# Fused transformer blocks, one core: the modulation rows are loaded into the weight ring instead of a buffer of their own

## The chip, the cores and the metric

The kernel is one program on one core of a Trainium2 chip. The metric is the device time of one execution in microseconds (us). The engines are named as in the profile: PE (TensorE, matmul), PEld (its weight load), DVE (VectorE), ACT (ScalarE), POOL (GpSimd), SP (SyncE, which here issues DMAs only). A wait on a semaphore holds everything that is queued behind it on its engine.

## The reference

Two blocks in a row in float32, on 512 tokens x and 256 context tokens with 1024 channels. The first has two layers: gated linear attention with differential attention, then a state-space mixer, each with a SwiGLU network and layer norms. The second has a SwiGLU network, a mixer of window attention and a gated scan (HGRN), and another SwiGLU network. Each layer's inputs are shifted, scaled and gated by "modulation" vectors, products of two conditioning vectors with a wide matrix:

```python
mod_x = jax.nn.silu(c) @ mod_w[layer] + mod_b[layer]          # 1024 -> 6144, two layers
mod_c = jax.nn.silu(c_ctx) @ mod_w[layer] + mod_b[layer]
hx = x * (1.0 + scm_x) + shm_x
mix_c, mix_x = even_mixer(hc, hx, ...) or odd_mixer(...)
x = layer_norm(ALPHA * x + gm_x * mix_x, ln_g[layer, 0], ln_b[layer, 0])
x = layer_norm(ALPHA * x + gf_x * swiglu(x * (1.0 + scf_x) + shf_x, ...), ln_g[layer, 1], ln_b[layer, 1])
...
mod = (jax.nn.silu(c) @ w_ada[l] + b_ada[l]).reshape(B, N_MOD, 1, D)   # 1024 -> 9216
```

## The kernel before, in words

Everything is written by hand. `plan` makes one list of 2756 steps; each engine walks the whole list and emits its share of every step, so the list fixes each engine's order. Waits are on semaphores.

**Weights.** A weight matrix is used in *panels* of at most 128 x 1024 float32 (512 KB), 475 of them. A panel is loaded into one of the four slots of the ring `RW` (panel n into slot n mod 4). For float32 accuracy from fp32r matmuls it is split: ACT copies it, rounded, to `RWH` ("hi", line 121), then DVE or POOL subtracts to get the rest, `RWr` ("lo", line 124). DVE does the panels with n mod 3 = 0, POOL the others. PE waits for the lo part before the first matmul of a panel. SP issues the load of panel n when PE has done with panel n-4, strictly in the order of n. `upto` says how far the splits and loads may run ahead at a step: at most 4 panels ahead for SP and 2 (`AHEAD`) for the splits, and only once panel n-4 is left behind in the list. Inside four latency-critical stretches ("calm") splits are held back further. A split stands in the order of ACT, DVE and POOL like any other instruction, and waits there.

**Modulation rows.** The 21 blocks of 1024 modulation values take 8 *rows* each, 168 in all (96 of `mod_w`, 72 of `w_ada`). A row is a 128 x 1024 piece of the matrix, 512 KB, used as it is, unsplit, by four matmuls with two output rows (`Mod.tensor`). PE does a row in about 0.6 us; the records show eight matmuls for it. After 8 rows ACT copies the sums out (`rowb`), PE turns them and DVE adds the bias ("turn"). Rows have a ring of their own, `MW`, three deep (class `Rows`): row n is issued by SP once row n-3 is used.

Where the rows stand in the list: 16 at the very start, before anything can be modulated; 8 in each of the two recurrent parts of the linear attention ("gla"); 16 in the differential attention; 14 around the layer norm before the first network, 42 between the panels of that network, 8 around the norm before the state-space mixer, 8 around the next norm, 8 in the second network, 8 around each of the two norms before and after the third network, 16 in the scan, 8 around the last norm. Around a norm, half the tokens' last products ("tail") alternate with the norm of the other half and with single rows (`ln_then_head`, `post_then_head`, line 3374 on); what is left of the rows stands in one run just before the *head*: the first two or three panels of the next stage, opened together. The head therefore begins when all of its panels are split.

Of the kernel before, what the change touches and what calls it, by code (L numbers as in the profile page):

```python
# [32 lines left out]
class Book:  # L33
# [3 lines left out]
    def __init__(self, make):  # L37
        self.make, self.sems, self.values, self.now, self.owner = make, {}, {}, {}, {}
# [34 lines left out]
class Eng:  # L73
# [2 lines left out]

    def __init__(self, who, real, k):
        self.who, self.real, self.k, self.book, self.seen, self.event = who, real, k, k.book, {}, None
        self.done_hi = self.done_lo = self.done_in = self.done_row = 0

    def wait_ge(self, name, *key):
        if self.real is None:
# [130 lines left out]
class Weights:  # L213
# [1 line left out]


    def __init__(self, k):
        self.k, self.specs, self.asked, self.used, self.through = k, [], 0, {}, []
        self.counting, self.left, self.calm = False, {}, {}

    def panel(self, p, nk, *cuts):

        n = self.asked
        self.asked += 1
        width = sum(w_ for _, w_ in cuts)
        assert nk * width <= 1024
        if self.counting:
            self.specs.append((nk, width, cuts))
        p.wait_ge(self.lo_name(n), n)
        fl = slice(0, nk * width)  # L230
        i = n % 4
        return n, *(x[:, i, fl].rearrange("p (k n) -> p k n", k=nk) for x in (self.k.RWH, self.k.RWL))

    def upto(self, i, ahead):


        n = self.through[i]
        while n < len(self.specs) and n < self.through[i] + 4 and ahead and self.left.get(n - 4, -1) < i - (
                self.calm.get(i, 0) if ahead < 4 else 0):
            ahead -= 1  # L240
            n += 1
        return n

# [3 lines left out]
    def fetch(self, y, upto):  # L247
        while y.done_in < min(upto, len(self.specs)):
            n = y.done_in
            y.done_in += 1  # L250
            nk, width, cuts = self.specs[n]
            if n >= 4:
                y.wait_ge(*self.used[n - 4])
            raw = self.k.RWF[:, n % 4, 0:nk * width].rearrange("p (k n) -> p k n", k=nk)
            at = 0
            for src, w_ in cuts:
                y.dma(raw[:, :, at:at + w_], src).then_inc(f"w.in{n % 4}", n, by=16)
                at += w_

    def split_hi(self, s, upto):  # L260
        while s.done_hi < min(upto, len(self.specs)):
            n = s.done_hi
            s.done_hi += 1
            nk, width, _ = self.specs[n]
            i, fl = n % 4, slice(0, nk * width)
            if n >= 4:
                s.wait_ge(*self.used[n - 4])
            s.wait_ge(f"w.in{i}", n)
            s.copy(self.k.RWH[:, i, fl], self.k.RWF[:, i, fl]).then_inc("w.hi", n)

    def split_lo(self, e, upto):
        while e.done_lo < min(upto, len(self.specs)):
            n = e.done_lo
            e.done_lo += 1
            if self.lo_name(n) != f"w.lo_{e.who}":
                continue
            nk, width, _ = self.specs[n]
            i, fl = n % 4, slice(0, nk * width)
            e.wait_ge("w.hi", n)
            e.tt(self.k.RWL[:, i, fl], self.k.RWF[:, i, fl], self.k.RWH[:, i, fl].bitcast(F),  # L280
                 ALU.subtract).then_inc(self.lo_name(n), n)


class Rows:

    DEEP = 3

    def __init__(self, k):  # L290
        self.k, self.src, self.step = k, [], {}

    def fetch(self, y, at):
        while y.done_row < len(self.src):
            n = y.done_row
            if n >= self.DEEP:
                if self.step[n - self.DEEP] >= at:
                    return
                y.wait_ge("pe.row", n - self.DEEP)
            y.done_row += 1  # L300
            y.dma(self.k.MW[:, n % self.DEEP, :], self.src[n]).then_inc(f"mw.in{n % self.DEEP}", n, by=16)


def wp(w, c0, n, r0=0, nk=8):
# [3 lines left out]
class Stage:  # L308


    def tensor(self, p, step, *a):
        pass
# [184 lines left out]
class Mod(Stage):  # L497
# [4 lines left out]
    def __init__(self, k):  # L502
        self.k = k
        a = k.a
        self.todo = [(a["mod_w"][0], k.M0, c, 0, "mod_b", 0) for c in range(6)]
        self.todo += [(a["mod_w"][1], k.M1, c, 0, "mod_b", 48) for c in range(6)]
        self.todo += [(a["w_ada_2"][0], k.M2, c, 1, "b_ada", 0) for c in range(9)]
        self.at, self.turned = 0, 0
        k.rows.src = [w[128 * kk:128 * kk + 128, 1024 * c:1024 * c + 1024] for w, _, c, _, _, _ in self.todo for kk in range(8)]

    def some(self, n, upto=168):

# [14 lines left out]
    def tensor(self, p, step, i):  # L527
        k = self.k
        if step == "row":
            b, kk = divmod(i, 8)  # L530
            w, _, c, x, _, _ = self.todo[b]
            if kk == 0:
                k.banks.take(p, 1, "mod", b)
            raw = k.MW[:, i % k.rows.DEEP, :]
            p.wait_ge(f"mw.in{i % k.rows.DEEP}", i)
            p.wait_ge("s.cs", x)
            for j in range(4):
                last = p.mm(k.banks.of("mod", b)[32 * j:32 * j + 2, 0:256], k.CS[:, x, kk, :],
                            raw[:, 256 * j:256 * j + 256], kk == 0, kk == 7)
            last.then_inc("pe.row", i)  # L540
        else:
            pt = k.banks.take(p, 1, "mod_t", i)
            p.wait_ge("s.row", i)
            for q in range(2):
                last = p.tr(pt[:, 128 * q:128 * q + 128], k.rowb[:, q * 128:(q + 1) * 128])
            last.then_inc("pe.row_t", i)
# [2781 lines left out]
def among(steps, extra, first=0, last=None):  # L3328

    last = len(steps) if last is None else last  # L3330
    out, at = [], 0
    for i, step in enumerate(steps):
        out.append(step)
        while first <= i < last and at < len(extra) * (i - first + 1) // (last - first):
            out.append(extra[at])
            at += 1
    return out
# [11 lines left out]
def run(stage, step, part, *tiles):  # L3349
    return [(stage, step, part, kk) for kk in tiles]  # L3350
# [95 lines left out]
def plan(k, out):  # L3446

    a, PX = k.a, (X, C)
    pro, mod, scale = Prologue(k), Mod(k), ModScale(k)
# [38 lines left out]
    steps = among(ffn.steps(), [("mod", 104)] * 42)  # L3488
# [13 lines left out]
    steps = among(ffn.steps(), [("mod", 128)] * 8)  # L3502
    steps = among(steps, run(ln, "late", H0, *range(8)) + run(ln, "late", H1, *range(8)), 2, 18)
# [51 lines left out]
    steps = []  # L3555
    for entry in order:
        steps += {"mod": lambda: mod.some(1, entry[1]), "mod_end": lambda: mod.until(entry[1])}.get(
            entry[0] if isinstance(entry[0], str) else "", lambda: [entry])()
    k.rows.step = {step[2]: i for i, step in enumerate(steps) if step[0] is mod and step[1] == "row"}
    for stage, names, n in ((diff, ("score",), 10), (ssd, ("cin", "yd"), 0), (hgrn, ("l2", "l3"), 24), (window, ("score",), 0)):  # L3560
        at = [i for i, step in enumerate(steps) if step[0] is stage and step[1] in names]
        k.w.calm.update((i, n) for i in range(at[0], at[-1]))
# [53 lines left out]
def sync_program(y, k, order, only=None):  # L3616
    for i in only or range(len(order)):
        stage, *step = order[i]
        if stage != "mark":
            stage.sync(y, *step)  # L3620
            k.rows.fetch(y, i)
            k.w.fetch(y, k.w.upto(i, 4))


# [18 lines left out]
def program(nc, a, con, out):  # L3643
    with ExitStack() as held:
        def sb(name, shape, dt=F):
            return held.enter_context(nc.sbuf_tensor(name, shape, dt))

        def sb2(name, shape):
            with nc.sbuf_tensor(name, shape, F) as f:
                pass  # L3650
            return f, sb(name + "r", shape, FR)
        k = Kernel()
# [4 lines left out]
        k.RWF, k.RWL = sb2("RW", [128, 4, 1024])  # L3657
        k.RWH = sb("RWH", [128, 4, 1024], FR)
        k.A, k.AR = sb2("A", [128, 18432])
        k.MW = sb("MW", [128, Rows.DEEP, 1024])  # L3660
        k.TM = sb("TM", [128, 4896])
        k.VEC = sb("VEC", [128, 5, 128])
        k.CS = sb("CS", [128, 2, 8, 2])
# [10 lines left out]
        PS = held.enter_context(nc.psum_tensor("PS", [128, 4096], F))  # L3674
        k.epsc, k.onec = k.cols[:, 0:1], k.cols[:, 1:2]
        k.ident, k.triF, k.triB, k.perm = (k.CC[:, i, :] for i in range(4))
        at = [0]
# [14 lines left out]
        k.acc = ([k.TM[:, 3072 + 512 * i:3584 + 512 * i] for i in range(2)], [k.TM[:, 4096:4352]])  # L3692
        k.sq_g = SqSet([k.TM[:, 4608:4864]], col(16))
        k.book = Book(lambda name: held.enter_context(nc.semaphore(name)))
        k.banks, k.w, k.rows, k.marks = Banks(PS), Weights(k), Rows(k), {}
        order = plan(k, out)

        count(k, order)
        block = held.enter_context(nc.Block())

        @block.sync
        def _(eng):
            sync_program(Eng("y", eng, k), k, order)
# [68 lines left out]
```

## Time and profile before

| | us |
|---|---|
| median of 3 runs | 4278.09 (4273.23 to 4280.25) |
| profiled execution | 4278.09 |
| its span | 4276.3 |
| PE busy in the span | 3870.9 (91%) |
| DVE, ACT, POOL busy | 1634.0, 1419.5, 1146.7 |
| mean granted clock of TensorE | 0.937 |

PE is busy for most of the span and carries most of the chain of waits; a change matters where PE waits. The DMA engines move 79 GB/s in the mean, in bursts around the norms.

### The profile page before, as it was taken

The page shows a single profiled execution, that of the slowest core. Times are in us where ns is not written, and L with a number is a line of the kernel's source. Part 1 is how long each engine was busy: PE and PEld are TensorE (multiplying, and loading weights), DVE is VectorE, ACT ScalarE, POOL GpSimd, SP SyncE. Part 2 cuts the span into 40 slices and gives each one's busy share as a digit, 9 for nine tenths or more (in the row PEclk, how much of TensorE's full clock was granted, in tenths as well). Part 3 has the DMA queues.
Part 4 walks back from the last instruction along what each step waited for, and adds up shares of the span by engine and source line. Part 5 has one row for each costly group of instructions (what it writes and reads, how often), then busy time and mean ns, then how long its engine had stood idle before and what let it go on. Part 6 is the DMA issues. An engine that isn't in the chain of part 4 may idle for free.

```text
span 4276.3 us, 52557 instructions
## 1 busy us (share of the span) xinstructions
PE 3870.9 (91%) x22131; PEld 3232.9 (76%) x22131; DVE 1634.0 (38%) x2831; ACT 1419.5 (33%) x2221; POOL 1146.7 (27%) x713
## 2 busy tenths in 40 slices
PE   5989878999998888888899989999978889898999
PEld 3767756888887677777778878888867676587888
DVE  2344454111135655646621241011247745332113
ACT  3222444212125223232432352221245535443223
POOL 1100003111123224231522341211333423243323
PEclk8989989999998898989899989999979989899999
DMA  4221124333332010111243332222232211143333
GB/s 160 69 76 40 40 79 128 99 104 99 104 113 75 25 50 30 50 36 45 79 123 108 100 114 68 65 65 65 74 108 60 60 46 38 33 123 99 95 98 109
DMA packets 471926, 336.69 MB, mean 79 GB/s; under 512 B 17530, under 2 KB 445580, under 8 KB 471692
## 3 DMA queue, kind: packets, MB, share of 16 engines
q1 hardware_dynamic: 471691, 333.34, 25.7%
q8 instruction: 175, 2.87, 0.3%
q14 instruction: 60, 0.48, 0.0%
HBM read 331.20 MB, written 2.10 MB: 78 GB/s over the span
## 4 chain that ended last, share of the span: by engine, by line
PE 76%; DVE 10%; ACT 4%; POOL 3%; DMA 3%; issue 3%; SPq 0%; POOLq 0%; DVEq 0%; ACTq 0%
PE PS L107 75%; DVE A L132 2%; PE PS L115 2%; DVE A L124 2%; DMA MW<-in_mod_w 1%; POOL RWr L124 1%; POOL TM L124 1%; ACT RWH L121 1%; DVE TM L132 1%; ACT A L118 1%; POOL A L124 1%; DVE TM L124 1%; ACT L118 1%; DVE RWr L124 1%; DVE XT L124 0%
## 5 line engine op out<-in xcount | busy, mean ns | idle before, releaser
L124 POOL TENSOR_TENSOR RWr<-RW,RWH 128x1024 fp32r<-128x1024 f32 (+2 forms) x316 | 725.3, 2297 | 2342.6 <-ACT RWH L121 2342.1
L107 PE MATMUL PS<-HTH,RWH 128*128 128x512 f32 (+3 forms) x3376 | 1222.0, 362 | 38.9 <-DVE HTr L124 14.1
L107 PE MATMUL PS<-HTr,RWH 128*128 128x512 f32 (+3 forms) x3376 | 1194.6, 354 | 0.0
L107 PE MATMUL PS<-HTH,RWr 128*128 128x512 f32 (+3 forms) x3376 | 1192.7, 353 | 0.0
L107 PE MATMUL PS<-Ar,RWH 128*128 128x512 f32 (+1 forms) x3264 | 828.1, 345 | 18.7 <-POOL Ar L124 8.7
L107 PEld LDWEIGHTS PS<-HTH,RWH 128*128 128x128 f32 (+2 forms) x3376 | 652.0, 193 | 164.5 <-issue 54.6
L107 PEld LDWEIGHTS PS<-HTH,RWr 128*128 128x128 f32 (+2 forms) x3376 | 650.6, 193 | 88.1 <-issue 1.3
L107 PEld LDWEIGHTS PS<-HTr,RWH 128*128 128x128 f32 (+2 forms) x3376 | 652.8, 193 | 82.3 <-issue 1.7
L107 PEld LDWEIGHTS PS<-Ar,RWH 128*128 128x128 f32 x3264 | 569.6, 193 | 111.2 <-issue 30.3
L121 ACT ACTIVATE RWH<-RW 128x1024 fp32r<-128x1024 f32 (+3 forms) x475 | 475.6, 1005 | 407.8 <-DMA RW<-in_ffn_w_out 180.2
L107 PE MATMUL PS<-Ar,RWr 128*128 128x512 f32 (+1 forms) x1632 | 556.5, 341 | 0.0
L124 DVE TENSOR_TENSOR A<-A,PS 128x512 f32<-128x512 f32 (+2 forms) x192 | 139.0, 724 | 820.4 <-PE PS L107 786.6
L124 DVE TENSOR_TENSOR RWr<-RW,RWH 128x1024 fp32r<-128x1024 f32 (+3 forms) x159 | 203.5, 1280 | 634.6 <-ACT RWH L121 634.5
L107 PE MATMUL PS<-A 128*128 128x128 f32 (+5 forms) x1692 | 326.5, 358 | 70.8 <-DVE A L124 32.5
L107 PEld LDWEIGHTS PS<-Ar,RWr 128*128 128x128 f32 x1632 | 315.0, 193 | 34.3
L107 PEld LDWEIGHTS PS<-A 128*128 128x128 f32 (+1 forms) x1692 | 233.3, 211 | 133.7 <-issue 68.5
L118 ACT ACTIVATE A<-PS 128x768 f32<-128x768 f32 (+2 forms) x148 | 93.0, 631 | 559.1 <-PE PS L107 549.7
L121 ACT ACTIVATE Ar<-A 128x512 fp32r<-128x512 f32 (+2 forms) x132 | 90.9, 689 | 546.6 <-DVE A L124 527.8
L132 DVE SCALAR_TENSOR_TENSOR XT<-PS,M,XT 128x512 f32<-128x512 f32 (+1 forms) x200 | 118.9, 619 | 337.1 <-PE PS L107 337.1
L118 ACT ACTIVATE A<-A 128x512 f32<-128x512 f32 (+4 forms) x144 | 103.1, 729 | 321.6 <-DVE A L132 146.8
L121 ACT ACTIVATE A<-PS 128x256 f32<-128x256 f32 (+5 forms) x200 | 104.0, 545 | 298.8 <-PE PS L107 217.8
L118 ACT ACT_TABLE_LOAD x137 | 175.8, 1283 | 34.0 <-PE PS L107 31.0
(181 smaller groups left out, 3783.2 us busy)
## 6 DMA issues: line engine op xcount, KB each, us to landing
RW<-in_ffn_w_in SPq DMA_DIRECT2D x176, 512.0 KB, 3.8
MW<-in_mod_w SPq DMA_DIRECT2D x96, 512.0 KB, 4.7
MW<-in_w_ada SPq DMA_DIRECT2D x72, 512.0 KB, 4.4
RW<-in_ffn_w_out SPq DMA_DIRECT2D x64, 512.0 KB, 3.7
RW<-in_ffn_w_out SPq DMA_DIRECT2D x64, 384.0 KB, 3.2
RW<-in_mix_w_in SPq DMA_DIRECT2D x41, 512.0 KB, 3.8
RW<-in_ssd_w_in SPq DMA_DIRECT2D x40, 512.0 KB, 4.0
RW<-in_ev_w_in SPq DMA_DIRECT2D x24, 512.0 KB, 3.9
```

What stands on the lines that cost most here:

```text
L107: return self._ins(self.real and self.real.matmul(o, l, r, start=start, stop=stop, skip_group_check=True))
L115: return self._ins(self.real and self.real.transpose(o, i, self.k.ident[0:n, 0:n]))
L118: return self._ins(self.real and self.real.activation(o, i, f, **kw))
L121: return self._ins(self.real and self.real.activation(o, i, ACT.Copy))
L124: return self._ins(self.real and self.real.tensor_tensor(out=o, in0=i0, in1=i1, op=op))
L132: return self._ins(self.real and self.real.scalar_tensor_tensor(out=o, in0=i0, scalar=sc, in1=i1, op0=op0, op1=op1))
```

## The change

The ring `MW` and the class `Rows` go. A row is now a "plain" panel of the ring `RW`: it takes the next number, its slot, its place in SP's order, and is not split. Panels and rows together are 643 entries. A plain entry doesn't count against the two or four entries that a split or load may run ahead, but it holds its slot. Which engine makes the lo part still goes by n mod 3, with the new numbers: 155 panels on DVE instead of 159, 320 on POOL instead of 316. The last edit drops an argument that sets the size of a DMA scratch area.

```diff
+    def whole(self, p, src, width):
+        n = self.asked
+        self.asked += 1
+        if self.counting:
+            self.specs.append((1, width, ((src, width),)))
+            self.plain.add(n)
+        p.wait_ge(f"w.in{n % 4}", n)
+        return n, self.k.RWF[:, n % 4, 0:width]
...
         n = self.through[i]
         while n < len(self.specs) and n < self.through[i] + 4 and ahead and self.left.get(n - 4, -1) < i - (
                 self.calm.get(i, 0) if ahead < 4 else 0):
-            ahead -= 1
+            ahead -= n not in self.plain
             n += 1
...
+            if n in self.plain:
+                continue
...
-            if self.lo_name(n) != f"w.lo_{e.who}":
+            if n in self.plain or self.lo_name(n) != f"w.lo_{e.who}":
                 continue
...
-class Rows:
...
-    DEEP = 3
...
-    def fetch(self, y, at):
-        while y.done_row < len(self.src):
...
-            raw = k.MW[:, i % k.rows.DEEP, :]
-            p.wait_ge(f"mw.in{i % k.rows.DEEP}", i)
+            num, raw = k.w.whole(p, w[kk * 128:kk * 128 + 128, c * 1024:c * 1024 + 1024].rearrange(
+                "(k p) n -> p k n", k=1), 1024)
             p.wait_ge("s.cs", x)
...
             last.then_inc("pe.row", i)
+            k.w.used[num] = ("pe.row", i)
...
-            k.rows.fetch(y, i)
             k.w.fetch(y, k.w.upto(i, 4))
...
-        k.MW = sb("MW", [128, Rows.DEEP, 1024])
...
-    nc = _bacc.Bacc("TRN2", target_bir_lowering=False, num_devices=1, dynamic_dma_scratch_size=1024)
+    nc = _bacc.Bacc("TRN2", target_bir_lowering=False, num_devices=1)
```

PE's order is the same but for the buffer's name. ACT's order at the start of the program, before (-) and now (+): `XT` are the tokens, `RWH` the hi part of a panel, `rowb` the sums of eight rows.

```order
-L121 ACTIVATE RWH<-RW 128x256
-L121 ACTIVATE RWH<-RW 128x1024
 L118 ACTIVATE XT<-PS 128x512 x8
 L118 ACTIVATE XT<-PS 128x256 x8
-L121 ACTIVATE rowb<-PS 2x256 x8
+L121 ACTIVATE rowb<-PS 2x256 x4
+L121 ACTIVATE RWH<-RW 128x256
+L121 ACTIVATE RWH<-RW 128x1024
+L121 ACTIVATE rowb<-PS 2x256 x4
```

The first two splits stood ahead of the tokens' copies; they now stand between the two blocks' sums.

SP's order before the first network (norm "f0"), before the change: `in_ev_w_out` is the tail, `in_ffn_w_in` the head and the network, `in_mod_w` the rows.

```order
L104 DMA RW<-in_ev_w_out 128x2x512 x2
L104 DMA MW<-in_mod_w 128x1024
L104 DMA RW<-in_ev_w_out 128x2x512
L104 DMA MW<-in_mod_w 128x1024 x5
L104 DMA RW<-in_ev_w_out 128x2x512
L104 DMA MW<-in_mod_w 128x1024 x5
L104 DMA RW<-in_ffn_w_in 128x8x128 x2
L104 DMA MW<-in_mod_w 128x1024 x3
L104 DMA RW<-in_ffn_w_in 128x8x128
```

The same place now:

```order
L104 DMA RW<-in_mod_w 128x1024 x10
L104 DMA RW<-in_ev_w_out 128x2x512 x3
L104 DMA RW<-in_mod_w 128x1024 x4
L104 DMA RW<-in_ev_w_out 128x2x512
L104 DMA RW<-in_mod_w 128x1024 x10
L104 DMA RW<-in_ffn_w_in 128x8x128 x2
L104 DMA RW<-in_mod_w 128x1024
```

The head's two panels were issued with ten or more rows still to come; they are now issued after the last of them.

SP's order before the second network (norm "f1"), before the change: `in_ssd_w_out` is the tail, `in_w_ada` the rows.

```order
L104 DMA RW<-in_ssd_w_out 128x4x256 x8
L104 DMA MW<-in_w_ada 128x1024
L104 DMA RW<-in_ffn_w_in 128x8x128
L104 DMA MW<-in_w_ada 128x1024 x2
L104 DMA RW<-in_ffn_w_in 128x8x128
L104 DMA MW<-in_w_ada 128x1024 x2
```

And now:

```order
L104 DMA RW<-in_ssd_w_out 128x4x256 x5
L104 DMA RW<-in_w_ada 128x1024 x2
L104 DMA RW<-in_ssd_w_out 128x4x256
L104 DMA RW<-in_w_ada 128x1024 x2
L104 DMA RW<-in_ssd_w_out 128x4x256
L104 DMA RW<-in_w_ada 128x1024 x2
L104 DMA RW<-in_ssd_w_out 128x4x256
L104 DMA RW<-in_w_ada 128x1024 x2
L104 DMA RW<-in_ffn_w_in 128x8x128 x8
```

The tail's panels were all issued ahead of the rows; now two rows stand before each of the last three, and all rows before the head.

## Rows read from the trace of the kernel before

**Rows 1.** The page's chain that ended last, share of the span by engine

```profile
PE 76%; DVE 10%; ACT 4%; POOL 3%; DMA 3%; issue 3%; SPq 0%; POOLq 0%; DVEq 0%; ACTq 0%
```

**Rows 2.** Instructions that use MW, whole span: who waited (us, times), and the landings

```profile
  PEld PS L107: 60.1, 28
  PE PS L107: 41.5, 27
...
DMA to landing us min/median/max: 3.4/4.5/12.1
```

**Rows 3.** Timeline, 9 to 64 us: start, length, engine, operation, count [idle before <-releaser]

```profile
25.08 1.06 ACT L121 ACTIVATE RWH<-RW 128x1024 fp32r<-128x1024 f32 x1 [1.37 <-DMA RW<-in_ev_w_in]
...
26.68 3.86 PE L115 MATMUL PS<-CC,A 128*128 128x128 f32 x16 [5.03 <-ACT XT L118]
...
30.46 1.48 PE L107 MATMUL PS<-MW,CS 128*2 128x256 f32 x24
31.14 28.33 SPq L104 DMA_DIRECT2D MW<-in_mod_w  x16
35.05 0.61 PE L107 MATMUL PS<-MW,CS 128*2 128x256 f32 x8 [3.11 <-DMA MW<-in_mod_w]
36.30 0.61 PE L107 MATMUL PS<-MW,CS 128*2 128x256 f32 x8 [0.64 <-DMA MW<-in_mod_w]
...
59.14 1.53 ACT L121 ACTIVATE rowb<-PS 2x256 f32<-2x256 f32 x4 [14.15 <-PE PS L107]
```

**Rows 4.** Timeline of PE, linear attention's recurrence, first block and second

```profile
148.19 1.03 PE L107 MATMUL PS<-MW,CS 128*2 128x256 f32 x8 [4.15 <-DMA MW<-in_mod_w]
...
149.16 2.08 PE L107 MATMUL PS<-A 64*128 64x256 f32 x8
...
152.98 1.13 PE L107 MATMUL PS<-A 64*128 64x256 f32 x8
...
156.52 0.61 PE L107 MATMUL PS<-MW,CS 128*2 128x256 f32 x8 [1.86 <-DMA MW<-in_mod_w]
...
280.35 1.03 PE L107 MATMUL PS<-MW,CS 128*2 128x256 f32 x8 [3.36 <-DMA MW<-in_mod_w]
```

**Rows 5.** First network, 700 to 1260 us: groups, then DMA issues to landing

```profile
L124 POOL TENSOR_TENSOR RWr<-RW,RWH 128x1024 fp32r<-128x1024 f32 x37 | 88.6, 2393 | 405.9 <-ACT RWH L121 405.9
...
L121 ACT ACTIVATE RWH<-RW 128x1024 fp32r<-128x1024 f32 x56 | 58.9, 1051 | 114.4 <-DMA RW<-in_ffn_w_out 64.3 <-DMA RW<-in_ffn_w_in 50.0
...
L124 DVE TENSOR_TENSOR RWr<-RW,RWH 128x1024 fp32r<-128x1024 f32 x19 | 23.2, 1222 | 92.9 <-ACT RWH L121 92.9
...
RW<-in_ffn_w_in SPq DMA_DIRECT2D x40, 512.0 KB, 3.9
```

**Rows 6.** Timeline of PE around the norm f0, 655 to 691 us

```profile
661.69 0.28 PE L107 MATMUL PS<-Ar,RWr 128*128 128x256 f32 x1
...
663.90 0.61 PE L107 MATMUL PS<-MW,CS 128*2 128x256 f32 x8
664.44 0.50 PE L107 MATMUL PS<-Ar,RWH 128*128 128x256 f32 x2
...
676.81 1.03 PE L107 MATMUL PS<-MW,CS 128*2 128x256 f32 x8
...
689.70 0.80 PE L107 MATMUL PS<-HTH,RWH 128*128 128x512 f32 x1
```

**Rows 7.** Timeline of PE: first matmuls of two of the state-space norm's tail panels

```profile
1273.14 0.50 PE L107 MATMUL PS<-Ar,RWH 128*128 128x256 f32 x2
...
1294.60 0.50 PE L107 MATMUL PS<-Ar,RWH 128*128 128x256 f32 x2
```

**Rows 8.** Timeline around the head after the norm f1, 2103 to 2114 us

```profile
2105.24 0.61 PE L107 MATMUL PS<-MW,CS 128*2 128x256 f32 x8
...
2105.92 1.53 ACT L121 ACTIVATE rowb<-PS 2x256 f32<-2x256 f32 x4 [2.42 <-PE PS L107]
...
2110.67 1.99 ACT L121 ACTIVATE RWH<-RW 128x1024 fp32r<-128x1024 f32 x2
...
2113.33 0.55 PE L107 MATMUL PS<-HTH,RWH 128*128 128x256 f32 x1 [6.84 <-DVE RWr L124]
```

**Rows 9.** Stretches: us, busy of the engines, granted clock of PE, DMA share, GB/s

```profile
690.00:1260.00 570.00, 564.30 (x3360) 475.92 (x3360) 109.26 (x152) 131.01 (x176) 108.69 (x53) 1.00 0.31 99
```

More of the change, by code:

```diff
@@ L78, in __init__ @@
         self.who, self.real, self.k, self.book, self.seen, self.event = who, real, k, k.book, {}, None
-        self.done_hi = self.done_lo = self.done_in = self.done_row = 0
+        self.done_hi = self.done_lo = self.done_in = 0
     def wait_ge(self, name, *key):
@@ L217, in __init__ @@
     def __init__(self, k):
-        self.k, self.specs, self.asked, self.used, self.through = k, [], 0, {}, []
+        self.k, self.specs, self.asked, self.used, self.through, self.plain = k, [], 0, {}, [], set()
         self.counting, self.left, self.calm = False, {}, {}
+    def whole(self, p, src, width):
[6 more added lines that the diff above has]
+        return n, self.k.RWF[:, n % 4, 0:width]
     def panel(self, p, nk, *cuts):
@@ L281, in split_lo @@
                  ALU.subtract).then_inc(self.lo_name(n), n)
-class Rows:
-    DEEP = 3
-    def __init__(self, k):
-        self.k, self.src, self.step = k, [], {}
-    def fetch(self, y, at):
-        while y.done_row < len(self.src):
[L295 to L301, printed above, removed]
 def wp(w, c0, n, r0=0, nk=8):
@@ L508, in __init__ @@
         self.at, self.turned = 0, 0
-        k.rows.src = [w[128 * kk:128 * kk + 128, 1024 * c:1024 * c + 1024] for w, _, c, _, _, _ in self.todo for kk in range(8)]
     def some(self, n, upto=168):
@@ L3558, in plan @@
             entry[0] if isinstance(entry[0], str) else "", lambda: [entry])()
-    k.rows.step = {step[2]: i for i, step in enumerate(steps) if step[0] is mod and step[1] == "row"}
     for stage, names, n in ((diff, ("score",), 10), (ssd, ("cin", "yd"), 0), (hgrn, ("l2", "l3"), 24), (window, ("score",), 0)):
@@ L3694, in program @@
         k.book = Book(lambda name: held.enter_context(nc.semaphore(name)))
-        k.banks, k.w, k.rows, k.marks = Banks(PS), Weights(k), Rows(k), {}
+        k.banks, k.w, k.marks = Banks(PS), Weights(k), {}
         order = plan(k, out)
```

## The prediction

> **What bounds the kernel now.** The page's chain first: three quarters of it are PE [rows 1]. So an edit counts where it makes PE wait or stops it waiting, and DMAs, splits and copies count only if PE stands for them. Next, who waits for the rows: PE 41.5 us in 27 waits, with landings of 3.4 to 12.1 us, median 4.5 [rows 2]. The weight loads' figure beside it is mostly the same idle time seen from PEld, and isn't added. In the timeline these waits lie where rows stand close together: 12.4 us in the first 16 rows, 10.9 us in the linear attention, and the rest in the runs of rows in front of heads. Last, the stretch table: in the first network PE is busy for 564.3 of 570 us at full granted clock [rows 9]; there is nothing to win there, only to lose. The profiled execution took 4278.09 us, 1.8 us more than its span, and is the median of the three runs, so changes are added to it directly.
>
> **The price of a slot.** Everything below uses one chain, from PE's last use of a slot to the first matmul of the panel that takes it: SP's issue 0.2 us (SP's row at 31.14 follows PE's first row, 30.46 plus 0.5, by that), landing 3.9, hi part 1.05, lo part 2.4 on POOL or 1.2 on DVE [rows 3, 5], and 0.3 for three semaphores, my estimate from the same rows. That is 7.85 us with POOL, 6.65 with DVE. A row needs 4.1. Loads issued together land 1.25 us apart (36.30 minus 35.05) [rows 3]. Before, four panels were in this chain beside three rows; now four entries of both kinds are.
>
> **The start: -10.** Before, ACT's first two splits stood ahead of the tokens' copies. ACT waited for their panels until 25.08, PE for ACT 5.03 us, so its last transposes ran from 26.68 and the first row at 30.46 [rows 3]. Now no split stands there. PE's 32 transposes of x ended at 26.68 - 5.03 = 21.65; eight steps for the context follow at 0.3 us each, so rows begin at about 24.1. That is 6.4 us sooner, and four rows are there instead of three. Row 4 is issued at 24.9, lands at 29, and rows 5 to 7 land 1.25 us apart, at 32.9. Then PE waits 2.3 us for the turn, as before. Rows 8 to 11 are there by then; rows 12 to 15 land from 41.0 to 44.8. The last sum is ready at 45.5 instead of 59.1: -13.6. But between the two `rowb` copies ACT now has two splits. The second's panel is issued once row 13 is used (42.9) and lands at about 47.9; with the copy that makes 49.0, so 3.5 us come back: -10. Bounds -14 (ACT isn't held up) and -5 (the panels land later than rows do; before, the second came only just ahead of 25.08).
>
> **Linear attention: -7.** The rows stand in pairs there. Before, the fourth row waits 4.15 us, as only three were loaded ahead, and after this wait the row takes 1.03 us and the next eight matmuls 2.08 instead of 1.13; the eighth waits 1.86. The second block repeats it (3.36 for the fourth row) [rows 4]. With four slots the fourth row is loaded when the last panel before it is done, at about 140.7, and comes 1.4 us late; the fifth and sixth are late by 1 us each. So 3.5 to 4 of each block's 5 to 6 us go. Bounds -11 (all waits go) and -3. The panel behind the last pair takes the slot of the fifth row; its 7.85 us end just when PE arrives.
>
> **The norm f0: +12.** Read [rows 6] by slots. Tail panel A, last used at 661.69 + 0.28 = 661.97, is followed by row r4 (663.90) in its slot: r4 lands at 661.97 + 4.1 = 666.1, late by 2.2. Panel B (wanted at 664.44) has the slot of an earlier row but stands behind r4 in SP's order: it lands at 667.3, and with hi and POOL is ready at 670.9, another 4.2 late. r8 (676.81) has B's slot; B ends at 676.9 + 6.4 = 683.3, so r8 comes at 687.4, 4.2 late. Six rows follow in one run; they waited 5.1 us before, and with r8's delay and four slots they still end near 695. The head's panels have the slots of the third- and second-last but one of them: the first is ready at 699.5, the second, on POOL too, at 702.0. PE began the head at 689.70: +12.3. Low bound +6: PE had small waits for the other half's norm in the head, and the norm's own chain may hide part. High bound +17: ACT stands behind B's split for 3 to 4 us with the first half's norm behind it.
>
> **State-space norm: +6.** Tail panels of 384 KB alternate with rows, seven first matmuls from 1273.14 to 1294.60, so one per 3.58 us [rows 7]. Now two panels and two rows fill the ring, so two panels take 2.4 us of matmuls and a chain of about 6.3 (0.2, 3.2, 0.8, 1.8 and 0.3, scaled by size from [rows 5]): 4.35 per panel. That is 0.8 x 6 = 4.6; the head's second panel adds 1 to 2. Bounds +3 and +9.
>
> **The norm f1: +9.** Two rows between the last tail panels: the panel wanted at about 2095.5 has the slot of the row that ends at 2090.9 and needs 7.85 us: 3 late; its neighbours about 1.5 and 0.7: +5. The head then hangs on ACT: last row 2105.24, `rowb` 2105.92, four norm copies, two splits 2110.67, DVE, head at 2113.33 [rows 8]. The first of these splits now stands ahead of `rowb` and its panel, in the slot of the last tail panel (2105.3), lands at 2109.4; `rowb` starts at 2110.5 instead of 2105.9. Hence +4 to +5. Bounds +3 and +13.
>
> **Norms b1, mix2, b2: +4, +4, +3.** Each has a run of five or six rows and then a head of two or three panels in these rows' slots. From the third-last row's end the second panel needs 7.85 us, in which the two remaining rows take 2.5: 5.3, less about 1 which the fourth slot saves in the run. b2's head already waited for a split of its third panel, so less. Bounds +1 and +7 each. **The scan:** 16 rows as singles; one panel's split is now placed one step ahead of its use, behind ACT's and DVE's backlog (+2, bounds 0 and +5), and the 2.5 us of waits for rows there shrink (-1). **Differential attention:** a stall of 3 us before a wait of equal length for ACT, 0 (bounds 0 and +4).
>
> **The first network: 0.** 42 rows between panels. With 56 wide splits in 560 us [rows 5] a panel lasts at most 10 us, by the stretch table some 8.5. At the 17 tightest places the slot's last use and the new panel's turn have one panel and two rows between them, 8.5 + 1.2 = 9.7 against 7.85. Slack 1.8 us, so nothing. DVE/POOL shares, four panels moved: 0. The scratch argument: it sets a reserve for another way of issuing than SP's, and all loads here are SP's: 0.
>
> **Sum.** -10 - 7 - 1 = -18; 12 + 6 + 9 + 4 + 4 + 3 + 2 = +40. 4278 - 18 + 40 = **4300 us**.
>
> **A rule of the skill on the chain.** The landing row says 3.9 us for 512 KB [rows 5]. The Trainium skill (DMA: Bandwidth & Descriptors, Anatomy of one DMA) gives, for loads issued by GpSimd, about 2.0 us fixed plus the bytes at 436 GB/s, an estimate of 3.2 us for this load. By it each of some twelve stalls would be 0.7 us shorter, and the sum about 4292; the trace has even its quickest row at 3.4, so I keep 3.9. The spacing of 1.25 us agrees with that bandwidth (1.2).
>
> **Rivals.** (1) *The stalls cost clock too.* After a wait of 4.15 us a row takes 1.03 us instead of 0.61 and eight matmuls 2.08 instead of 1.13, so some 1.4 us more per such wait [rows 4]. Six new waits of that size in the tails: +8, 4308. Against it: in the tails before, some matmuls already ran at the lower clock, and half my waits are shorter. The Trainium skill (TensorE: Matmul & The Clock Gate, Part 1: The HAM clock gate) has idle gaps drop the engine from 2.4 to 1.2 GHz; the trace's two durations agree. Chance 0.13. (2) *The ring is short in the first network as well*: ACT's or POOL's other work uses up the 1.8 us at the 17 places, 1 to 1.5 us each: +20, 4320. For it: ACT is now held for the landing there, with evictions behind it. Against: 114.4 us of ACT's idle time there was waiting for DMA anyway [rows 5]. Chance 0.10. (3) *Stalls hidden by the norms*: PE would have stood for the other half's norm anyway, as at the 6.84 us before f1's head [rows 8]. If half the +40 goes: 4280. Against: that wait's chain itself begins with the last row and its split. Chance 0.17. (4) *Faster.* The start and the linear attention give their bounds (-14, -11) and the stalls at the heads stay under +15, because the norms before the heads, not the ring, end last: 4278 - 25 + 15 = 4268. It decides at +16 of stalls (4269). Against it: f0 alone is 6 at its least. Chance 0.08. (5) That the change doesn't do what it says: SP's order shows that it does. The forecast keeps 0.52.
>
> **Range and chances.** A measurement of this kernel tells about 0.2% (8.6 us) from no change. 4300 with terms moving together spans 4286 to 4312; (1) and (2) reach beyond it above, (3) below. 4276 to 4318 leaves out half of (2), most of (4) and little else. Slower by over 0.2% (above 4286.6): 0.50 of the forecast, (1), (2) and a little of (3), 0.75. Faster by over 0.2% 0.08, within 0.17.
>
> **What would show it.** The first row of PE at about 24 us, the attention's first product some 10 us sooner; PE's waits before the fourth row in the linear attention down to 1 to 2 us. In the tails: PE's matmuls of panels with waits for POOL RWr or DVE RWr, ACT's RWH with waits for DMA RW of 2 to 5 us; each head's first matmul later against its last row than before. In 700 to 1260 us PE still over 98% busy. I am wrong if the heads' distances are unchanged (then 4 holds), or if PE waits for RWr all through the first network (2).

## The result, and the profile after

The kernel after takes 4319.56 us (median of 4 runs, 4318.03 to 4333.61), the kernel before 4275.66 in the same comparison. The ratio is 1.0116 with a 95% interval of 1.0085 to 1.0149: 36 to 64 us slower. The forecast was 4300. The ratio rests on three more executions of after besides these four; all seven lie between 4313.16 and 4345.09. The profiled execution of after is the slowest of the four (span 4331.1); a second trace of the same order of work, taken in experiment e13, has a span of 4319.8 and is read beside it.

The page's chain answers to [rows 1]; PE's share is one point lower, DVE's one higher:

```profile
PE 75%; DVE 11%; ACT 4%; DMA 3%; POOL 3%; issue 3%; SPq 0%; POOLq 0%; DVEq 0%; ACTq 0%
```

Who waits for `RW`, whole span (it holds the rows now, so this is not the same set as [rows 2]):

```profile
  PEld PS L107: 142.7, 62
  PE PS L107: 105.4, 48
...
DMA to landing us min/median/max: 2.7/3.8/12.9
```

The start, for [rows 3] (timeline: start, length, engine, operation, idle before and its releaser):

```profile
23.26 1.91 PE L107 MATMUL PS<-RW,CS 128*2 128x256 f32 x32
28.01 0.61 PE L107 MATMUL PS<-RW,CS 128*2 128x256 f32 x8 [2.85 <-DMA RW<-in_mod_w]
...
46.70 0.42 ACT L121 ACTIVATE RWH<-RW 128x256 fp32r<-128x256 f32 x1 [12.27 <-DMA RW<-in_ev_w_in]
48.41 1.06 ACT L121 ACTIVATE RWH<-RW 128x1024 fp32r<-128x1024 f32 x1 [1.29 <-DMA RW<-in_ev_w_in]
49.49 1.53 ACT L121 ACTIVATE rowb<-PS 2x256 f32<-2x256 f32 x4
```

The first row comes at 23.26 instead of 30.46, the second `rowb` at 49.49 instead of 59.14. The first network answers to [rows 9] and is unchanged:

```profile
702.00:1272.00 570.00, 564.42 (x3365) 476.19 (x3365) 109.72 (x153) 137.06 (x178) 111.99 (x54) 1.00 0.34 98
```

So the time is in the norms: f0, the state-space norm and f1, then b1 (before the third network), mix2 (before the last mixer) and b2 (before the last network). The stretch view over the six of them, cut at the same instructions in both kernels (from the first matmul of the tail's second half to the head's first or, for the state-space norm, last tile), shows it best. The columns that matter are the length, PE busy with its count, and the granted clock (third from the end). Before:

```profile
644.93:689.70 44.77, 36.74 (x252) 23.98 (x250) 27.58 (x42) 15.87 (x24) 22.71 (x18) 0.84 0.59 185
1268.64:1326.38 57.74, 49.02 (x330) 38.79 (x328) 30.16 (x48) 27.59 (x45) 29.91 (x24) 0.86 0.46 139
2056.63:2113.33 56.70, 44.85 (x328) 38.50 (x329) 29.91 (x60) 22.92 (x39) 33.86 (x28) 0.80 0.45 149
2490.74:2523.46 32.72, 23.01 (x184) 17.13 (x185) 8.42 (x20) 14.14 (x28) 15.42 (x15) 0.87 0.59 182
3100.99:3135.47 34.48, 28.98 (x204) 23.77 (x205) 14.03 (x20) 16.01 (x28) 17.92 (x12) 0.80 0.59 183
3848.08:3879.93 31.85, 22.75 (x201) 19.36 (x201) 10.85 (x20) 15.27 (x32) 16.29 (x13) 0.84 0.48 149
```

After:

```profile
635.82:701.69 65.87, 40.97 (x252) 27.98 (x250) 23.68 (x39) 15.09 (x23) 20.83 (x17) 0.68 0.44 144
1279.49:1342.79 63.30, 49.60 (x330) 38.66 (x328) 29.94 (x47) 28.51 (x46) 32.60 (x25) 0.87 0.43 125
2069.54:2144.11 74.57, 50.48 (x329) 42.94 (x329) 29.51 (x59) 22.85 (x40) 35.98 (x29) 0.73 0.37 113
2522.48:2565.70 43.22, 28.43 (x184) 22.17 (x185) 8.48 (x19) 17.34 (x34) 15.52 (x16) 0.65 0.55 161
3145.43:3192.10 46.67, 33.82 (x205) 27.84 (x205) 17.47 (x27) 17.66 (x29) 19.52 (x13) 0.67 0.46 125
3892.76:3934.55 41.79, 25.47 (x200) 21.59 (x200) 10.95 (x19) 17.19 (x36) 16.89 (x14) 0.76 0.53 151
```

The six last 258.3 us before and 335.4 after, 77.2 more. For the same matmuls PE is busy 205.4 us before and 228.8 after: 23.4 of the 77.2 is slower work, at a clock of 0.65 to 0.76 instead of 0.80 to 0.87 in five of six; 53.8 is waiting. In the second trace of this order the same sums are 322.9 and 221.3: 64.6 more, 16.0 of it slower work and 48.6 waiting. Outside the norms 21 to 22 us come back in both traces.

Where the same PE work starts in each trace, against before's trace, gives a ledger by part (us later; e14 and e15 have the rows of f0 or f1 alone in the ring, e5 and e1 are the kernel after with five and seven slots):

| part | forecast | after | e13 | e14 | e15 | e5 | e1 |
|---|---|---|---|---|---|---|---|
| up to f0's tail | -17 | -9.1 | -14.6 | +2.5 | -2.7 | -22.3 | -27.5 |
| f0 | +12 | +21.1 | +18.8 | +17.6 | -0.6 | +11.4 | +11.9 |
| first network | 0 | -1.1 | -1.2 | +0.4 | +0.2 | +0.5 | +1.4 |
| state-space norm | +6 | +5.5 | +5.9 | -1.1 | +0.1 | -1.3 | -3.2 |
| state-space stage | 0 | -3.5 | -3.5 | +0.1 | -0.8 | -19.6 | -17.3 |
| f1 | +9 | +17.9 | +16.5 | +0.1 | +15.1 | +17.4 | +7.8 |
| b1 | +4 | +10.5 | +6.4 | +1.1 | +4.9 | +3.2 | +0.2 |
| mix2 | +4 | +12.2 | +6.8 | -0.4 | -0.1 | +6.0 | +3.9 |
| scan, window | +1 | -11.9 | -6.3 | -0.1 | -3.1 | +2.6 | +1.4 |
| b2 | +3 | +9.9 | +10.2 | +0.4 | -0.1 | +3.2 | +6.9 |

The columns e14 and e15 also show how far a part without an edit moves from one execution to the next: mostly 1 us, up to 5. The second and third network (after +0.9 and +2.2) are left out. A norm's term can be cut once more, at the end of its last row. What is added behind it, up to the head's first matmul, is in after and e13 7.0 and 7.9 us at f0, 4.4 and 4.1 at f1, 8.3 and 6.6 at b1, 7.8 and 7.2 at mix2, 4.2 and 3.7 at b2; the rest of each term lies in the tail.

The chain through f0 says why its term grew (start, length, what; for [rows 6]):

```profile
659.25 2.35 POOL RWr L124
661.60 0.04 issue
661.65 15.70 PE PS L107 x80
677.34 0.02 issue
677.36 4.15 DMA RW<-in_mod_w
...
682.65 4.45 DMA RW<-in_mod_w
...
687.61 7.74 DMA RW<-in_ffn_w_in
...
695.71 1.06 ACT RWH L121
696.77 0.07 issue
696.84 4.65 POOL RWr L124 x2
```

The rows land after 4.15 and 4.45 us, as reckoned; the head's panel, issued behind rows, after 7.74 where 3.9 was reckoned. It is so at the head of b1 (DMA issues, 2545 to 2562 us: KB each, median us to landing), where the same form in the network has 3.9 [rows 5]:

```profile
RW<-in_ffn_w_in SPq DMA_DIRECT2D x4, 512.0 KB, 7.5
RW<-in_w_ada SPq DMA_DIRECT2D x3, 512.0 KB, 3.7
```

At f1, for [rows 8] (timeline):

```profile
2123.04 0.80 PE L107 MATMUL PS<-Ar,RWH 128*128 128x256 f32 x2 [4.35 <-POOL RWr L124]
...
2135.55 1.06 ACT L121 ACTIVATE RWH<-RW 128x1024 fp32r<-128x1024 f32 x1 [7.71 <-DMA RW<-in_ffn_w_in]
2136.51 1.51 ACT L121 ACTIVATE rowb<-PS 2x256 f32<-2x256 f32 x4
...
2144.11 0.55 PE L107 MATMUL PS<-HTH,RWH 128*128 128x256 f32 x1 [11.14 <-DVE RWr L124]
```

The split stands ahead of `rowb` and waits for its load, as foretold; from the last row (2131.22) to the head are 12.9 us instead of 8.1. The other 13 us of f1 are in its tail.

### The profile page after: what moved, and what is told of

Read it like the earlier page. It is cut to its first block, busy times and chain, and to the rows that moved or that the text cites. A ratio compares the mean times of both kernels' runs of the same rounds, so it can differ in the third digit from the quotient of the medians.

```text
span 4331.1 us, 52592 instructions
## 1 busy us (share of the span) xinstructions
PE 3884.8 (90%) x22131; PEld 3244.0 (75%) x22131; DVE 1647.4 (38%) x2827; ACT 1426.7 (33%) x2221; POOL 1156.3 (27%) x717
## 4 chain that ended last, share of the span: by engine, by line
PE 75%; DVE 11%; ACT 4%; DMA 3%; POOL 3%; issue 3%; SPq 0%; POOLq 0%; DVEq 0%; ACTq 0%
PE PS L107 73%; DVE A L124 3%; DVE A L132 2%; PE PS L115 2%; POOL RWr L124 1%; POOL TM L124 1%; DMA RW<-in_mod_w 1%; DMA RW<-in_ffn_w_in 1%; ACT RWH L121 1%; DVE TM L132 1%; POOL A L124 1%; DVE TM L124 1%; ACT A L118 1%; DVE RWr L124 1%; DVE SM L144 0%
## 5 line engine op out<-in xcount | busy, mean ns | idle before, releaser
L124 POOL TENSOR_TENSOR RWr<-RW,RWH 128x1024 fp32r<-128x1024 f32 (+3 forms) x320 | 733.0, 2293 | 2438.2 <-ACT RWH L121 2432.7
L107 PE MATMUL PS<-Ar,RWH 128*128 128x512 f32 (+1 forms) x3264 | 838.9, 348 | 35.8 <-POOL RWr L124 17.6
L107 PEld LDWEIGHTS PS<-Ar,RWH 128*128 128x128 f32 x3264 | 579.2, 196 | 131.9 <-issue 26.3
L124 DVE TENSOR_TENSOR RWr<-RW,RWH 128x1024 fp32r<-128x1024 f32 (+2 forms) x155 | 199.9, 1290 | 648.4 <-ACT RWH L121 648.2
L118 ACT ACT_TABLE_LOAD x137 | 175.8, 1283 | 36.3 <-PE PS L107 33.2
```

What stands on the lines that cost most here:

```text
L107: return self._ins(self.real and self.real.matmul(o, l, r, start=start, stop=stop, skip_group_check=True))
L118: return self._ins(self.real and self.real.activation(o, i, f, **kw))
L124: return self._ins(self.real and self.real.tensor_tensor(out=o, in0=i0, in1=i1, op=op))
```

## The experiments

The theories: **A**, rows hold slots that panels need. **B**, one queue in strict order costs, whatever the depth. **C**, the lo parts' new engines. **D**, ACT and POOL stand at splits with the norm's work behind them. **Q**, loads queue behind loads. Differences below are in us against the kernel before on the same chip, from the ratio, with its 95% interval.

**e1, seven slots.** The hi buffers stay four, taken in turn by panels alone, and the scratch argument is as before in e1 and e5 (e13 shows that it is worth nothing). Of the edit the lines that set the number are shown; the rest makes the slot `n % RING` (e5 has `RING = 5`).

```diff
+RING = 7
...
-        k.RWF, k.RWL = sb2("RW", [128, 4, 1024])
+        k.RWF, k.RWL = sb2("RW", [128, RING, 1024])
```

> The kernel after, with seven slots for the raw data of the shared ring (the memory that the row buffer had), and still four hi buffers, which the panels alone take in turn. One numbering and one order of loads stay. Theory A (too few slots: every row in a tail or a head's run takes a slot that a panel's load needed) expects that the loss of 44 us goes and the gain at the start and in the linear attention stays: 4258 to 4272, and the heads' first matmuls as far behind the last row as before. Theory B (one queue of loads in strict order of use is what costs, however many slots) expects 4300 or more. Theory C (which engine makes the lo part, since the numbers changed) expects 4305 to 4325.

Measured: 4260.12, **-10.7** (-15.4 to -6.4). With the memory of the row buffer put into the ring the loss in time is gone, though numbering and order are those of after. B and C fall as the main cause of it. But the loss in the norms is not gone, as the sums of the stretch view over the six of them show, first e5 (below), then e1:

```profile
sum 298.27, PE 209.94 PEld 165.81 DVE 119.77 ACT 117.25 POOL 135.77; mean PE 34.99 PEld 27.63 DVE 19.96 ACT 19.54 POOL 22.63
sum 285.77, PE 213.38 PEld 169.28 DVE 121.04 ACT 113.52 POOL 138.69; mean PE 35.56 PEld 28.21 DVE 20.17 ACT 18.92 POOL 23.11
```

Against 258.3 before, the norms are 27.5 us longer with seven slots and 40.0 with five, where four cost 65 to 77. The kernel is faster all the same because 27.5 us are won ahead of f0 and 17.3 in the state-space stage (ledger). The heads' first matmuls are again as far behind the last row as before at f1, mix2 and b2, as expected, but not at f0 (12.8 us more) and b1 (6.2 more). The chain of e1 into the head of f0:

```profile
653.41 9.14 DMA RW<-in_ffn_w_in
...
662.64 0.04 ACT RWH L122
...
663.60 0.81 ACT HTH L119
...
671.64 2.32 POOL RWr L125
```

The panel is issued early and lands late, behind other loads (Q), and the norm's copy `HTH` stands behind its split on ACT (D). More slots cure neither.

**e5, five slots.**

> The kernel after with five slots for the raw data instead of four (seven gave 4260). Theory A (a panel's load waits for a slot that a row holds): the tails, where panels and rows alternate one to one, need one slot more, and the heads' panels are issued one row sooner; well over half of the 60 us between four and seven slots come back: 4275 to 4290. If the loss were spread evenly over the three slots, 4300.

Measured: 4278.08, **+1.3** (-3.8 to 6.0). Against the runs' own comparisons the first slot more brings 42 to 48 us and the next two together 12 (by the bare times 42 and 18). A holds for the greater part: one slot more takes 25 to 37 us off the norms, most of it in the tails, and adds 8 to 13 to the lead ahead of f0. The 16 us more in the state-space stage have no experiment.

**e2, the lo part's engine by the count of panels.** The edit: `lo_name` counts panels without the rows.

> The kernel after, with the lo part's engine chosen by the count of panels alone, as before the change (159 on DVE, 316 on POOL, the same panels as before). Theory C (both panels of the first network's head fell to POOL, 4.6 us in a row instead of 2.4 beside 1.2): 3 to 8 us of the 44 come back, 4312 to 4317. Theory A: 4316 to 4322, the panels come late because of their slots and the engine of the lo part moves only some of the heads.

Measured: 4322.06, **+50.8** (41.9 to 59.4). C falls for the whole.

**e3, splits stand later.**

```diff
-            ahead -= n not in self.plain
+            ahead -= 1 if split else n not in self.plain
```

> The kernel after, with rows counted against the two entries that a split may stand ahead of its use: the splits of a head stand behind more of the rows and of the norm's own work in the order of ACT, POOL and DVE; loads are issued as in the kernel after. Theory D (ACT and POOL stand in front of a split whose load has just been issued, and the norm's squares and copies queue behind it: the half of the loss that the prediction did not have): 4295 to 4308. Theory A (the load itself is late): 4318 to 4330, since a split that stands later cannot be ready sooner.

Measured: 4315.14, **+45.3** (36.3 to 54.7), the loss of after within the interval. That speaks against D only where the edit moved a split, which is outside the norms and in the tails from the state-space norm on. Around f0 the order of ACT, DVE and POOL in the trace is that of after, and at f1, b1, mix2 and b2 two splits still stand ahead of `rowb`. ACT at the head of f1 in e3:

```profile
2131.48 1.06 ACT L121 ACTIVATE RWH<-RW 128x1024 fp32r<-128x1024 f32 x1 [6.62 <-DMA RW<-in_ffn_w_in]
2132.45 1.52 ACT L121 ACTIVATE rowb<-PS 2x256 f32<-2x256 f32 x4
```

So D was not tested at the heads, and there the traces show it at work: in after `rowb` begins 4.3 us behind the end of the last row at f1, 4.0 at mix2 and 4.3 at b2, each time held by a split that waits for its load; before it was 0.1. That is all that the heads of f1 and b2 lose and half of what mix2's loses.

**e4, e8, e10, the first rows alone.** Only rows below 32 or 16 go through `whole`, the others keep `MW`; in e10 the lo parts keep their engines of before too.

> The kernel before, with only rows 0 to 31 (start and linear attention) in the weight ring; all the others keep their own buffer of three. All theories: the gain of the first part alone. By the prediction 17 us (10 at the start, 7 in the linear attention), 4259; by the trace of the kernel after 10 to 11 us (the linear attention's gain was given back behind its second block), 4265. If the loss of 44 us sits in the tails and heads alone, this one is faster than before; if the shared ring costs in the linear attention too, 4266 to 4270.

> The kernel before, with only rows 0 to 15 (the start) in the weight ring (rows 0 to 31 gave 4258). The prediction has 10 us for the start and 7 for the linear attention; the traces have the start at 10 and next to nothing for the linear attention, where DVE's chain takes the place of the rows that are no longer waited for (PE waits 5 to 8 us for it in the second block). By the prediction 4263 to 4265; by the traces 4257 to 4260, the same as with rows 0 to 31.

> Rows 0 to 31 in the weight ring as in the run with 4258, with the lo part's engine chosen by the count of panels alone, so that every panel has the engine that it has in the kernel before. Theory S: 4256 to 4260 as with the shifted numbers. Theory N: 4264 to 4269, of which the start and the linear attention are all.

Measured: e4 4257.62, **-15.4** (-21.4 to -9.4); e8 4271.31, **-3.4** (-8.6 to 1.7); e10 4264.38, **-8.1** (-14.1 to -2.6). With every lo part on its engine of before, the start and the linear attention together are worth 8 (3 to 14), not 17. e4's other 7 are not clear of the noise; in its trace they lie in the state-space stage (-14.1 against e10's -1.9) and the scan, so they may belong to the shifted lo parts. e8 missed its expectation, and its gain is not clear of nothing. That not all of the linear attention's waits are won is seen in the chain of the kernel after through its second recurrence:

```profile
271.92 5.04 DMA RW<-in_ev_w_in
...
277.04 1.06 ACT RWH L121
278.10 0.02 issue
278.12 0.03 DVE RWr L124
...
280.21 0.34 DVE A L132
```

The panel behind the last pair of rows has a row's slot; DVE stands at its lo part until 278.12, with the recurrence's own steps queued behind it, and PE then waits 5.17 us for `A`. Before, it did not wait there. With seven slots (e1) the same wait is 7.69 us.

**e9, e12, the turn of DVE and POOL by itself.** `n % 3 == 1` or `== 2` in the kernel before.

> The kernel before, but DVE makes the lo part of the panels with n mod 3 = 1 instead of 0 (158 panels against 159); nothing else. Rows 0 to 31 in the ring gave 15 us, rows 0 to 15 gave 4, while in their traces both start equally early; what differs behind the linear attention is the numbers alone, shifted by 32 (so DVE has what was n mod 3 = 1) and by 16 (n mod 3 = 2). Theory N (the turn of DVE and POOL matters in the scans and the state-space stage, and the shifted numbers gave the rest): 4262 to 4268. Theory S (the turn is of no account, the linear attention is what made the 11 us): 4272 to 4280.

> The kernel before, but DVE makes the lo part of the panels with n mod 3 = 2 instead of 0; nothing else. It is the turn that panels behind the start have with rows 0 to 15 in the ring (4271). Theory N: this turn costs against that of before, 4279 to 4285, and explains why the start alone brought 4 and not 9 us. Theory S: 4272 to 4280.

Measured: e9 4272.46, **-4.7** (-9.0 to -0.4); e12 4276.66, **+0.9** (-4.7 to 6.0). Over the whole kernel the turn is worth little. In a part of it it can be worth more, as the next pair shows.

**e6, e14, f0's rows alone**, with shifted and with unshifted lo parts.

> The kernel before, with only rows 48 to 61 (the tail and head at the norm before the first network) in the weight ring. The trace of the kernel after has PE 21.6 us later over this stretch, where the prediction had 12. If the stretch by itself costs this, 4273 + 20 = 4293 (4288 to 4298); if half of it is only the start's gain given back (other engines were not earlier than before, so that PE waits for them again), 4273 + 12 = 4285.

> The kernel before with rows 48 to 61 in the weight ring, and every panel's lo part on its engine of before. If the term of f0 was right (12): 4288 (4284 to 4290). If it was mis-sized as the traces have it (17 to 21, since the head's panels land after 7.7 us): 4293 to 4297.

Measured: e6 4284.63, **+10.7** (6.8 to 14.5); e14 4299.23, **+22.7** (17.1 to 28.2). In the traces f0 itself costs nearly the same, 19.8 and 17.6 us. e6's trace gets 21 back in the state-space norm and stage, the third network and the scan, e14's nothing; 8 of the 21 is that e6's traced execution is its fastest (4276.43, median 4284.63). So e6's time, which seemed to confirm the term of 12, did so by other parts. The term is 17 to 21.

**e16, f0's rows with a quarter of the bytes** (the rest of each is left out).

```diff
+            if n in self.plain:
+                y.dma(raw[:, :, 0:256], cuts[0][0][:, :, 0:256]).then_inc(f"w.in{n % 4}", n, by=16)
+                continue
```

> As the run with rows 48 to 61 in the ring and the lo parts by the panel, but these 14 rows load only their first 256 of 1024 columns; the rest of each is left out. Theory Q (half of f0's cost is loads that stand in the queue behind other loads): 7 to 10 us less than with whole rows, 4284 to 4288. Theory A alone (slots held): 2 to 3 us less, from three rows that land 0.9 us sooner each.

Measured: 4289.06, **+15.0** (9.4 to 20.1), 7.7 less than e14; the f0 part itself is 12.5 instead of 17.6. The chains ahead of the head, e14 and then e16:

```profile
689.47 6.89 DMA RW<-in_mod_w
696.36 0.04 issue
696.41 0.66 PE PS L107 x8
697.06 0.02 issue
697.08 7.86 DMA RW<-in_ffn_w_in
```

```profile
683.24 2.12 DMA RW<-in_mod_w
...
691.86 6.10 DMA RW<-in_ffn_w_in
```

Rows land in 2.12 instead of 3.7 to 6.9, and the chain goes through the second head panel (6.10) instead of the first (7.86). Q holds for the rows' bytes: by the time in full, by the trace (5.1 us less at f0, where A alone had 2 to 3) in part. But the head's panels still land 6.6 us after issue in the median in both: they queue behind each other as well, which shorter rows don't change.

**e7, the same for all rows from 32 on.**

> The kernel after, but rows 32 to 167 load only their first 256 of 1024 columns (128 KB instead of 512), and PE multiplies these four times; the rest of each row is left out. The slots are held as before and the order is the same. Theory Q (in a run before a head the loads of rows and panels stand in one burst, so that the head's panels land after 7.4 us and not after the 3.9 of the network): the panels land sooner by the bytes of the two to three rows ahead of them, and the rows by their own 0.9 us each: 18 to 28 us of the 60 come back, 4292 to 4302. Theory A alone (slots, with landings of 3.9): only the rows' own landing gets shorter, some ten waits by 0.9: 4308 to 4313.

Measured: 4301.03, **+26.1** (20.5 to 31.6), so 18 to 24 less than after: Q's number. Here too the head's panels land after 5.6 to 6.0, not 3.9.

**e11, the runs ahead of four heads alone.**

> The kernel before, with only the rows that stand in one run ahead of the heads of f0, b1, mix2 and b2 in the weight ring (6, 6, 5 and 5 rows), and the lo parts on the engines of before. By the prediction the heads are 4 (b1), 4 (mix2), 3 (b2) and some 4 of f0's 12: 4275 + 15 = 4290. By the trace of the kernel after, whose head panels land 6.4 to 7.7 us after their issue instead of 3.9, each has 3 to 4 us more: 4275 + 28 = 4303 (4297 to 4308).

Measured: 4287.53, **+10.3** (5.6 to 15.0); in the trace f0 3.9, b1 2.7, mix2 6.4, b2 2.6, together 15.6. The number is the prediction's 15 and not my corrected 28, but it is so by two errors that cancel. From the last row to the head's first matmul PE loses 5.6, 6.1, 7.8 and 4.0 us, 23.5 together and nearly what the full change loses there (27.3 and 25.4 in its two traces), with first landings of 6.3 to 7.3 us in the chains; and the work up to the last row takes 7.9 us less than before in all (here the other rows still have their three slots, so there are more slots in all; that this is the reason is not tested). What the full change adds at these norms lies ahead of the last row, where single rows stand in the tails.

**e15, f1's rows alone.**

> The kernel before with rows 112 to 119 (the tail at f1) in the weight ring, lo parts on their engines of before. If the term of f1 was right (9): 4285. If it is as the trace of the kernel after has it (18): 4294. With the last tail panel's lo part on DVE, as here, and not on POOL as there, the trace with lo parts by the panel had 10: I take 4286.

Measured: 4291.05, **+19.7** (13.3 to 26.1), 15.1 in the part itself by the trace. Its chain has a tail panel that lands after 6.73 us behind the rows. The 4.9 us at b1, where nothing was edited, are slower work: PE is busy 29.8 us there instead of 23.0, at a clock of 0.62.

**e13, the scratch argument restored in the kernel after.**

> The kernel after with the argument for the DMA scratch area restored: this part alone is undone. All theories: no difference, 4320 (4314 to 4325), since every load is SP's. If the argument did cost something, 4310 or less. Its trace is a second one of the same order of work: f0 17 to 21 us, f1 10 to 18 by it, or the first trace misled.

Measured: 4319.32, **+43.2** (35.5 to 50.4), the time of after. This part of the change does nothing to the time.

**e17, e18, versions meant to be fast**: DVE's turn moved by one from row 48 on, with e10's and with e1's ring.

> Rows 0 to 31 in the weight ring, lo parts by the count of panels as in the run with 4264, but from row 48 on DVE has the panels with count mod 3 = 1. If the turn behind f0 is worth what the two pairs of runs show (7 and 14 us): 4250 to 4258. If it is not: 4262 to 4267. Faster than both kernels either way.

> Seven raw slots shared by rows and panels (4260), lo parts by the count of panels, from row 48 on with count mod 3 = 1 on DVE. If the turn is worth 7 to 14 us over that of before, and the turns of the run with seven slots were a mixture: 4250 to 4258; else 4260 to 4265.

Measured: e17 4257.91, **-21.8** (-28.3 to -15.8), faster than both kernels and the best against its own comparison, though its interval overlaps e4's; e18 4270.90, **-9.8** (-13.7 to -6.0), no better than e1. So the turn is no rule that carries over, and why it moves the state-space stage and the scan stays open.

## Why the prediction was wrong

The direction and the places were right, the size was half. By its steps:

- **Start, -10**: the trace has it (-9.7; `rowb` at 49.49 against about 49 foretold). In time the first 16 rows alone bring 3.4 (-8.6 to 1.7, e8) and the first 32 together 8.
- **Linear attention, -7**: failed. That the panel's 7.85 us "end just when PE arrives" was reckoned for PE alone; DVE stood at the split with the recurrence behind it. In the trace of after PE's lead was 9.6 us ahead of the part, 15.2 at its best and 8.3 at its end, so the part gave nothing; e8 and e10, without and with its rows in the ring, are both 9 us ahead at f0's tail. The differential attention, put at 0, took the lead to 17 and back to 9 (21 and 15 in e13); no experiment follows this up.
- **First network 0, state-space norm +6**: right (5.5 and 5.9).
- **Norm f0, +12**: mis-sized, 17 to 21, and 22.7 in time by e14. The first three waits were right to 0.4 us: 1.90, 4.55 and 4.23 against 2.2, 4.2 and 4.2. What failed is the price of a slot: 3.9 for a landing that took 7.74, because two rows and the next panel were in the queue. That is 4. The other 4 is PE at the lower clock between the waits.
- **Norm f1, +9**: mis-sized, 15 to 18. The head's share of 4 to 5 was right (4.8); the tail's 5 was 13, with waits of 2.7, 1.1 and 4.4 for POOL, landings of up to 6.7 us and slower work (5.6 us more busy time).
- **b1, mix2, b2, 4 + 4 + 3**: 23 to 33 together. The heads, which were all that was priced, lose 17 to 20 instead of 11: their panels land after 6.5 to 8.6 us instead of 3.9, and at mix2 and b2 `rowb` stands behind the split, as had been reckoned at f1 alone. The other 6 to 12 lie in the tails, whose single rows were given no price, though f0's steps two paragraphs earlier showed what such a row costs.
- **Rival 1, stalls cost clock, +8 at 0.13**: the right mechanism, wrongly kept apart. It goes with the waits, whatever they are, and made 16 to 23 us, one for every two to three us of new waiting. Behind the wait of 4.55 us at f0 the granted clock was 0.50, the level of 1.2 GHz, for the next 15.6 us, all of them busy (661.65 to 677.30); behind the wait of 4.35 at f1 it was 0.50 for the next 8.3. A row took 1.03 us there instead of 0.61. The Trainium skill (TensorE: Matmul & The Clock Gate, Part 1: The HAM clock gate) has idle time lower the clock from 2.4 to 1.2 GHz; the durations agree.
- **Scan, +1**: -6 to -12 in the traces. The turn of DVE and POOL, which the prediction put at 0, may have a share: e12 with another turn has -9.9 there, e9 -0.2. It is not settled.
- **The shorter landing**, which would have made the sum 4292, led the wrong way. The Trainium skill (DMA: Bandwidth & Descriptors, Queues, rings and completion order) has what was missing: on each DMA engine the descriptors of a ring are consumed in order. By that, a panel behind two rows that land 1.25 us apart comes 2.5 later than alone; the 7.74 and 7.86 against 3.9, and the fall in e16, agree in direction and exceed it. That the panels behind it take part is my reading and is not tested.

In sum 38 us of stalls were forecast for the six norms; 49 to 54 of waiting and 16 to 23 of slower work came, and some 22 went elsewhere: 43 to 55 in the two traces.

## What to carry to other kernels

Price a load that must arrive in time by its place in the queue, not by the median landing of a stretch where loads stand alone; a ring that is reloaded in a burst pays that at every head. Add to each new wait of a busy TensorE the slower work behind it, here a third to nearly a half of the wait. Sharing a ring is good where the parts need slots at different times: five shared slots take the time of four and three, and seven are 11 us faster, though the norms, where both parts need slots at once, still lose 27 us with seven. With a split engine that works in order, ask also what queues behind the split.

## What the runs showed of the hardware

- Loads of 512 KB in 4 KB pieces (rows) land 1.25 us apart when issued together; panels of 512-byte pieces 1.5 to 1.8 us apart (e14 and e16, by the splits that wait for them).
- The same order of work takes the six norms 335.4 us in one execution and 322.9 in another; 7 of the 12.5 is PE's busy time, by the clock. A part's cost read from one pair of traces is good to some 5 us.
- A lead is not kept: in e13's trace PE was 21 us ahead at 600 us and 15 at 645. e6 and e14, with the same edit to rows, differ by 12 us.
- Dropping the DMA scratch argument changed nothing here, where all loads are SP's (4319.32 against 4319.56).
